# Attention on one core: the order in which TensorE takes scores, transposes and values of the key chunks

## The chip, the cores and the metric

The kernel runs on one core of one Trainium2 chip. The metric is the device time of the whole program in microseconds, the median of several runs. Engines are named as in the profile: PE is TensorE's matmul stream and PEld its weight loads, DVE is VectorE, ACT is ScalarE, POOL is GpSimd, SP is the queue that issues the DMAs here.

## What is computed

One step of a decoder layer with two groups of heads. The part that the change touches is the attention of the 2048 new tokens: four heads, two softmax maps per head, whose difference weighs the values.

```python
def _diff_attend(q, k, v, q_pos, k_pos, lam):
    s = jnp.einsum('bqhmd,bshmd->bhmqs', q.astype(jnp.float32), k.astype(jnp.float32)) * (A_DQK ** -0.5)
    mask = k_pos[None, :] <= q_pos[:, None]
    s = jnp.where(mask, s, -jnp.inf)
    p = jax.nn.softmax(s, axis=-1)
    w = p[:, :, 0] - lam * p[:, :, 1]
    return jnp.einsum('bhqs,bshd->bqhd', w, v.astype(jnp.float32))
```

The sizes: SEQ 2048 in 16 tiles of 128 query rows, 4 heads, 64 columns per map of a query or key, 128 columns of a value, all float32.

## The kernel before

Four passes follow one another, each closed by a barrier of all engines: projections, attention (`pass_attention`), the decoding samples, and the output product. The change lies in the TensorE program of `pass_attention`.

The work is a row of 64 "heads" n = 0 to 63: 16 query tiles in the order of `TILES` (1, 3, ..., 15, then 14, 12, ..., 0; line 939), four heads each. Tile i sees (i + 1) x 128 keys, cut into chunks of up to 512 columns: 1 to 4 chunks; 16 of the 64 heads have 1, 16 have 2, 16 have 3 and 16 have 4. Three stages of the pipeline run in one iteration n:

- `scores(n, c)` (line 1177, matmuls on L1188) makes the scores of chunk c for both maps: six matmuls with 64 rows, three pairs, since float32 is split into a high and a low part (Q_hi K_hi, Q_hi K_lo, Q_lo K_hi). The two maps go to two of four PSUM buffers `sps`, so two chunks fill all four. It waits (L1184) until VectorE has read the two buffers that the chunk before the last one used.
- `weight_columns(n - 3, c)` (line 1193, L1201) transposes the weights of chunk c of head n - 3, 128x128 each, into one of two buffers `tps`; ScalarE copies it to one of two buffers `WT` (`weights_out`, L1087).
- `values(n - 3, c)` (line 1204, L1214) multiplies `WT` with V; each 128x128 block takes two matmul instructions. It waits for ScalarE's copy.

Before the scores of a "prepared" head (`prepared`, line 994: heads 1 to 3 of a tile while K still grows, head 1 later; 29 in all, 22 of them with two or more chunks), `prep` (L1174) transposes a tile of raw K or Q into the next `sps` buffer; ScalarE copies its high part (`split_hi`, L1072) and VectorE the low part (`split_lo`, L1110), which frees the buffer. The wait of `scores(n, 1)` counts this read too.

ScalarE's program in iteration n: `split_hi` of the prepared tile, the exponentials of map 0 of head n - 1 (`exp_row`, L1078), `weights_out(n - 3, 0)`, the exponentials of map 1, then the other `weights_out`. VectorE's: `combine(n - 2)` (L1140, the difference of the two maps over the whole row), `split_lo`, then `rows(n)`: for each chunk and map it reads the scores out of PSUM with scale, mask and running maximum (L1124), and at the end the negated maximum (L1129). Each engine runs its own queue in order.

In the loop at line 1226 TensorE takes, for each c, `scores(n, c)`, `weight_columns(n - 3, c)`, and `values(n - 3, c - 1)`.

Of the kernel before, what the change touches and what calls it, by code (L numbers as in the profile page):

```python
# [941 lines left out]
def pass_attention(nc, io, keep):  # L942


    with ExitStack() as ctx:
# [48 lines left out]
        def prepared(n):  # L994
            u, h = divmod(n, H)
            return tile_raw[u + 1][h - 1:h] if h and u + 1 < NP else ()
# [16 lines left out]
        def n_chunks(n):  # L1013
            return len(chunks[n // H]) if 0 <= n < n_heads else 0
# [11 lines left out]
        @block.sync  # L1026
        def _(sp):
            def load(r):
                if r >= 4:
                    sp.wait_ge(s["sps_full"], raw_use[r - 4] + 1)  # L1030
                kind, t = raw[r]
                sp.dma_start(qk_in[:, r % 4], io["k_p" if kind == "k" else "q_s"][t * P:(t + 1) * P, :]).then_inc(s["qk_load"][r % 4], 16)

            def store(u):
                sp.wait_ge(s["out"], u + 1)
                sp.dma_start(io["o_s"][TILES[u] * P:(TILES[u] + 1) * P, :], ob[:, u % 2]).then_inc(s["store"][u % 2], 16)

            def load_v(q):
                sp.dma_start(V[:, 4 * q:4 * q + 4, :], io["v_p"].rearrange("(b p) n -> p b n", p=P)[:, 4 * q:4 * q + 4, :])\
                  .then_inc(s[f"v_load{q}"], 16)  # L1040

            for r in range(3):
                load(r)
            sp.dma_start(mask[:, :], io["causal"]).then_inc(s["mask_load"], 16)
            load(3)
            load_v(0)
            at = 4
            for u in range(NP):
                if 1 <= u < 4:
                    load_v(u)  # L1050
                while at < len(raw) and at - 4 <= tile_raw[u][-1]:
                    load(at)
                    at += 1
                if u >= 1:
                    store(u - 1)
            store(NP - 1)
            for p in range(2):
                sp.wait_ge(s["store"][p], 16 * NP // 2)
# [107 lines left out]
        @block.tensor  # L1166
        def _(pe):
            def prep(r):
                k = raw_use[r]
                pe.wait_ge(s["qk_load"][r % 4], 16 * (r // 4 + 1))  # L1170
                if k >= 4:
                    pe.wait_ge(s["sps_read"], k - 3)
                for h in range(H):
                    mm = pe.transpose(sps[k % 4][:, h * P:(h + 1) * P], qk_in[:, r % 4, h * P:(h + 1) * P], ident[:, :])  # L1174
                mm.then_inc(s["sps_full"], 1)

            def scores(n, c):

                u, h = divmod(n, H)
                c0, w = chunks[u][c]  # L1180
                if c == 0:
                    pe.wait_ge(s["sps_read"], raw_use[tile_raw[u][-1]] + 1)
                k = first_sc[n] + 2 * c
                pe.wait_ge(s["sps_read"], k - 2)  # L1184
                for q, kk in ((Q_hi, K_hi), (Q_hi, K_lo), (Q_lo, K_hi)):
                    for m in range(2):
                        d = slice(m * DQ, (m + 1) * DQ)
                        mm = pe.matmul(sps[(k + m) % 4][:, 0:w], q[u % 2][d, h, :], kk[d, h, c0:c0 + w],  # L1188
                                       start=(q is Q_hi and kk is K_hi), stop=(q is Q_lo))
                        if q is Q_lo:  # L1190
                            mm.then_inc(s["sps_full"], 1)

            def weight_columns(n, c):
                g = first_wt[n] + c
                if c == 0:
                    pe.wait_ge(s["weights"], n + 1)
                if g >= 2:
                    pe.wait_ge(s["wT"], g - 1)
                c0, w = chunks[n // H][c]
                for b in range(w // P):  # L1200
                    mm = pe.transpose(tps[g % 2][:, b, :], sc[0][:, n % 4, c0 + b * P:c0 + (b + 1) * P], ident[:, :])  # L1201
                mm.then_inc(s["wT_ps"], 1)

            def values(n, c):
                u, h = divmod(n, H)
                g = first_wt[n] + c
                c0, w = chunks[u][c]
                pe.wait_ge(s["wT"], g + 1)
                pe.wait_ge(s[f"v_load{c}"], 16)
                if h == 0 and c == 0 and u >= 2:  # L1210
                    pe.wait_ge(s["out"], u - 1)
                for b in range(w // P):
                    kb = c0 // P + b
                    mm = pe.matmul(ops[u % 2][:, h, :], WT[:, g % 2, b, :], V[:, kb, h * DV:(h + 1) * DV],  # L1214
                                   start=(kb == 0), stop=(kb == TILES[u]))
                mm.then_inc(s["out_ps"], 1)


            for r in tile_raw[0]:
                prep(r)  # L1220
            for n in range(n_heads + 3):
                n_s, n_v = n_chunks(n), n_chunks(n - 3)
                if n < n_heads:
                    for r in prepared(n):
                        prep(r)
                for c in range(max(n_s, n_v + 1)):
                    if c < n_s:
                        scores(n, c)
                    if c < n_v:
                        weight_columns(n - 3, c)  # L1230
                    if 1 <= c <= n_v:
                        values(n - 3, c - 1)


def pass_samples(nc, io, keep):
# [660 lines left out]
```

## Time and profile before

| | |
|---|---|
| median of 3 runs | 1796.92 us (1795.34 to 1799.09) |
| profiled execution: time, span | 1799.58 us, 1797.8 us |
| PE busy in the span | 1609.2 us (90%) |
| PEld busy | 1299.9 us (72%) |
| DVE busy | 988.6 us (55%) |
| ACT busy | 754.3 us (42%) |
| attention stage | 1004.4 to 1394 us of the span |

Busy time is a share of a span with several stages of different limits; the attention stage is read by itself. Matmuls are pipelined, so the cadence of their starts says more than their durations. In a timeline, like instructions in a row are merged: "x4" starts at the first one's start.

### The profile page before, as it was taken

How to read it: one execution, taken by the hardware profiler on the slowest of the kernel's cores; microseconds unless marked ns; L12 is line 12 of the kernel's file. 1: busy time of each engine (PE TensorE's matmuls, PEld its weight loads, DVE VectorE, ACT ScalarE, POOL GpSimd, SP SyncE). 2: the span in 40 equal slices, each digit the busy share in tenths (PEclk: the TensorE clock that was granted, in tenths of full speed). 3: DMA queues.
4: the chain of work that ended last, by engine and by line, in shares of the span. 5: the costliest groups of instructions: out<-in, count | busy, mean ns of one | idle time of the engine just before them, and what ended most of it. 6: DMA issues, size and time to landing. Idle time of an engine off the chain costs nothing. (4 is left out here: it accounts for less than half of the span.)

```text
span 1797.8 us, 25182 instructions
## 1 busy us (share of the span) xinstructions
PE 1609.2 (90%) x9156; PEld 1299.9 (72%) x9156; DVE 988.6 (55%) x2314; ACT 754.3 (42%) x1076; POOL 495.1 (28%) x637
## 2 busy tenths in 40 slices
PE   7799999997999999999999699999998378599998
PEld 5588888886877878788787466777776245377776
DVE  5322222254776676677666498888887341343332
ACT  4333333345445345444544466666666022221110
POOL 1323333333446545644654000000000210012121
PEclk9999999998999999999999699999999589899999
DMA  8433333453001101010110430100000845324342
GB/s 294 173 141 141 141 140 141 175 190 115 30 30 54 36 30 52 31 36 30 54 36 7 152 118 25 47 14 13 13 18 25 254 160 191 107 100 164 134 152 70
DMA packets 79827, 172.27 MB, mean 96 GB/s; under 512 B 9059, under 2 KB 15715, under 8 KB 79715
## 3 DMA queue, kind: packets, MB, share of 16 engines
q1 hardware_dynamic: 79714, 170.79, 27.7%
q8 instruction: 69, 1.13, 0.3%
q14 instruction: 44, 0.35, 0.1%
HBM read 114.13 MB, written 56.62 MB: 95 GB/s over the span
## 5 line engine op out<-in xcount | busy, mean ns | idle before, releaser
L92 PE MATMUL h_banks<-h_w_hi,h_x_hi 128*128 128x512 f32 x1088 | 435.1, 400 | 24.0 <-DVE h_x_lo L651 16.8
L94 PE MATMUL h_banks<-h_w_hi,h_x_lo 128*128 128x512 f32 x1088 | 426.6, 392 | 0.0
L93 PE MATMUL h_banks<-h_w_lo,h_x_hi 128*128 128x512 f32 x1088 | 426.3, 392 | 0.0
L92 PEld LDWEIGHTS h_banks<-h_w_hi,h_x_hi 128*128 128x128 f32 x1088 | 206.3, 190 | 66.6 <-DVE h_x_lo L651 17.2
L94 PEld LDWEIGHTS h_banks<-h_w_hi,h_x_lo 128*128 128x128 f32 x1088 | 205.8, 189 | 44.5
L93 PEld LDWEIGHTS h_banks<-h_w_lo,h_x_hi 128*128 128x128 f32 x1088 | 206.4, 190 | 40.6
L145 POOL TENSOR_TENSOR h_stage_or_levels<-h_stage_or_levels,h_qk_or_hgrn 128x128 f32<-128x128 f32 x192 | 107.4, 559 | 278.2 <-ACT h_stage_or_levels L589 278.2
L1078 ACT ACTIVATE p_scores<-p_scores,p_nmx 128x256 f32<-128x256 f32 (+15 forms) x128 | 153.1, 1196 | 6.2 <-DVE p_nmx L1129 5.9
L1214 PE MATMUL p_ops<-p_V,p_WT 128*128 128x128 f32 x1088 | 146.4, 280 | 8.8 <-ACT p_WT L1087 8.4
L1214 PEld LDWEIGHTS p_ops<-p_V,p_WT 128*128 128x128 f32 x1088 | 132.6, 193 | 15.8 <-ACT p_WT L1087 14.4
L1124 DVE CUSTOM_DVE_ANT_0 p_scores<-p_sps,p_zero 128x512 f32<-128x512 f32 x192 | 122.2, 686 | 15.9 <-PE p_sps L1188 15.7
L737 DVE TENSOR_TENSOR h_qk_or_hgrn<-h_banks,h_mask 128x896 f32<-128x896 f32 x64 | 69.7, 1090 | 105.6 <-PE h_banks L877 105.6
L1087 ACT ACTIVATE p_WT<-p_tps 128x512 f32<-128x512 f32 (+3 forms) x160 | 84.7, 530 | 84.9 <-PE p_tps L1201 84.7
L83 PE MATMUL y_yps<-y_w_hi,y_mT_hi 128*128 128x512 f32 x272 | 111.3, 409 | 7.8 <-DVE y_yt L1764 6.4
L589 ACT ACTIVATE h_stage_or_levels<-h_stage_or_levels 128x2560 f32<-128x2560 f32 x32 | 75.1, 2346 | 102.5 <-DVE h_stage_or_levels L136 102.5
L741 DVE TENSOR_REDUCE h_qk_or_hgrn<-h_qk_or_hgrn 128x128 f32<-128x896 f32 x64 | 111.3, 1739 | 2.2
L876 PE MATMUL h_banks<-h_stage_or_levels 128*128 128x128 f32 x768 | 97.7, 277 | 15.9 <-POOL h_stage_or_levels L150 15.9
L876 PEld LDWEIGHTS h_banks<-h_stage_or_levels 128*128 128x128 f32 x768 | 93.1, 191 | 25.1 <-POOL h_stage_or_levels L150 22.6
L661 DVE TENSOR_REDUCE h_ss<-h_xs_sq_or_tok 128x8 f32<-128x512 f32 x34 | 21.7, 681 | 162.7 <-ACT h_xs_sq_or_tok L486 162.7
L1363 POOL MEMSET s_Q<- 128x1024 f32 x1 | 1.0, 952 | 395.1 <-POOLq L58 395.1
L83 PE MATMUL y_yps<-y_w_lo,y_mT_hi 128*128 128x512 f32 x272 | 108.9, 400 | 0.0
L83 PE MATMUL y_yps<-y_w_hi,y_mT_lo 128*128 128x512 f32 x272 | 108.7, 400 | 0.0
(218 smaller groups left out, 2739.3 us busy)
## 6 DMA issues: line engine op xcount, KB each, us to landing
h_stage_or_levels<-in_w_in SPq DMA_DIRECT2D x32, 512.0 KB, 6.3
h_xs_sq_or_tok<-in_xT SPq DMA_DIRECT2D x17, 512.0 KB, 6.0
h_qk_or_hgrn<-in_x SPq DMA_DIRECT2D x17, 512.0 KB, 6.1
tmp_xh_s<-h_x_hi SPq DMA_DIRECT2D x17, 512.0 KB
tmp_xl_s<-h_x_lo SPq DMA_DIRECT2D x17, 512.0 KB
h_x_hi<-tmp_xh_s SPq DMA_DIRECT2D x17, 512.0 KB, 3.6
h_x_lo<-tmp_xl_s SPq DMA_DIRECT2D x17, 512.0 KB, 4.5
s_kc<-in_cache_k SPq DMA_DIRECT2D x32, 256.0 KB, 3.8
```

The costliest lines, as they stand in the source:

```text
L83: mm = eng.matmul(out, a[:, k, :], b[:, k, cols], start=(k == 0 and a is x_hi and b is w_hi), stop=(k == KD - 1 and a is x_lo))
L92: eng.matmul(out, x_hi[:, k, :], w_hi[:, k, :], start=(k == 0), stop=False)
L93: eng.matmul(out, x_hi[:, k, :], w_lo[:, k, :], start=False, stop=False)
L94: mm = eng.matmul(out, x_lo[:, k, :], w_hi[:, k, :], start=False, stop=(k == KD - 1))
L145: pool.tensor_tensor(e_up, e_up, q_up, ALU.mult)
L589: act.activation(lv[hf], lv[hf], ACT.Exp).then_inc(s["decay"], 1)
L741: dve.tensor_reduce(att[:, h % 2], masked.rearrange("p l t -> p t l"), AX.X, ALU.add).then_inc(s["att"], 1)
L876: pe.matmul(lps[:, n, :], l[:, n, c], l[:, n, c], start=True, stop=True)
L1078: act.activation(row, row, ACT.Exp, bias=nmx[:, n % 2, m:m + 1], accum_out=ls[:, u % 2, m, h:h + 1]).then_inc(s["exp"], 1)
L1087: act.activation(WT[:, g % 2, 0:w // P, :], tps[g % 2][:, 0:w // P, :], ACT.Copy).then_inc(s["wT"], 1)
L1124: dve.tensor_tensor_reduce(sc[m][:, n % (4 - m), c0:c0 + w], sps[k % 4][:, 0:w], add, SCALE, -3e38, ALU.add, ALU.max, mx[:, n % 2, m, c:c ...
L1214: mm = pe.matmul(ops[u % 2][:, h, :], WT[:, g % 2, b, :], V[:, kb, h * DV:(h + 1) * DV], start=(kb == 0), stop=(kb == TILES[u]))
```

## The change

In iteration n, TensorE takes the chunks two at a time: the scores of chunks c0 and c0 + 1 first, then for these two chunks in turn the transposes of head n - 3 and the values of the chunk before. No instruction, buffer or wait differs.

```diff
-                for c in range(max(n_s, n_v + 1)):
-                    if c < n_s:
+                for c0 in range(0, max(n_s, n_v + 1), 2):
+                    for c in range(c0, min(c0 + 2, n_s)):
                         scores(n, c)
-                    if c < n_v:
-                        weight_columns(n - 3, c)
-                    if 1 <= c <= n_v:
-                        values(n - 3, c - 1)
+                    for c in (c0, c0 + 1):
+                        if c < n_v:
+                            weight_columns(n - 3, c)
+                        if 1 <= c <= n_v:
+                            values(n - 3, c - 1)
```

## Rows read from the trace of the kernel before

**Rows 1.** Attention stage's window (busy us per engine, clock, DMA); POOL group, page part 5.
```profile
1004.40:1394.00 389.60, 365.04 (x2720) 278.32 (x2720) 327.20 (x960) 251.66 (x449) 0.00 (x0) 0.97 0.13 43
...
L1363 POOL MEMSET s_Q<- 128x1024 f32 x1 | 1.0, 952 | 395.1 <-POOLq L58 395.1
```
**Rows 2.** Timeline of PE, head 38 (start us, us, engine, line, operation, count).
```profile
1258.47 0.50 PE L1188 MATMUL p_sps<-p_K_hi,p_Q_hi 64*128 64x512 f32 x2
1258.81 0.40 PE L1188 MATMUL p_sps<-p_K_lo,p_Q_hi 64*128 64x512 f32 x2
1259.04 0.39 PE L1188 MATMUL p_sps<-p_K_hi,p_Q_lo 64*128 64x512 f32 x2
1259.36 0.66 PE L1201 MATMUL p_tps<-ident,p_scores 128*128 128x128 f32 x4
1259.95 0.50 PE L1188 MATMUL p_sps<-p_K_hi,p_Q_hi 64*128 64x512 f32 x2
...
1261.34 1.06 PE L1214 MATMUL p_ops<-p_V,p_WT 128*128 128x128 f32 x8
...
1265.56 1.73 PE L1214 MATMUL p_ops<-p_V,p_WT 128*128 128x128 f32 x14
1267.22 0.51 PE L1188 MATMUL p_sps<-p_K_hi,p_Q_hi 64*128 64x512 f32 x2
```
**Rows 3.** Timeline of ACT, head 38: second exponential and the copy after it.
```profile
1260.55 1.67 ACT L1078 ACTIVATE p_scores<-p_scores,p_nmx 128x1664 f32<-128x1664 f32 x1
...
1262.22 0.59 ACT L1087 ACTIVATE p_WT<-p_tps 128x512 f32<-128x512 f32 x1
```
**Rows 4.** Timeline of head 58 (one score chunk, two value chunks), PE and ACT.
```profile
1375.03 0.77 PE L1201 MATMUL p_tps<-ident,p_scores 128*128 128x128 f32 x5
...
1375.72 0.60 ACT L1087 ACTIVATE p_WT<-p_tps 128x512 f32<-128x512 f32 x1 [1.42 <-PE p_tps L1201]
...
1376.37 1.38 PE L1214 MATMUL p_ops<-p_V,p_WT 128*128 128x128 f32 x10 [0.58 <-ACT p_WT L1087]
```
**Rows 5.** Timelines of PE and of DVE, prepared head 22.
```profile
1110.93 0.60 PE L1174 MATMUL p_sps<-ident,p_qk_in 128*128 128x128 f32 x4
...
1112.36 0.66 PE L1201 MATMUL p_tps<-ident,p_scores 128*128 128x128 f32 x4
1113.82 0.50 PE L1188 MATMUL p_sps<-p_K_hi,p_Q_hi 64*128 64x512 f32 x2 [0.80 <-DVE p_K_lo L1110]
...
1115.20 1.06 PE L1214 MATMUL p_ops<-p_V,p_WT 128*128 128x128 f32 x8
...
1111.34 1.82 DVE L1140 SCALAR_TENSOR_TENSOR p_scores<-p_scores,p_coef 128x1536 f32<-128x1536 f32 x1
1113.07 0.69 DVE L1110 TENSOR_TENSOR p_K_lo<-p_sps,p_K_hi 128x512 fp32r<-128x512 f32 x1
```
**Rows 6.** Timeline of PE, prepared head 45: preparation and second chunk's scores.
```profile
1310.52 0.60 PE L1174 MATMUL p_sps<-ident,p_qk_in 128*128 128x128 f32 x4
...
1312.53 0.50 PE L1188 MATMUL p_sps<-p_K_hi,p_Q_hi 64*128 64x512 f32 x2
```
**Rows 7.** Timeline of head 50 (two score chunks), PE and ACT.
```profile
1341.19 0.65 PE L1201 MATMUL p_tps<-ident,p_scores 128*128 128x128 f32 x4
...
1341.89 0.60 ACT L1087 ACTIVATE p_WT<-p_tps 128x512 f32<-128x512 f32 x1 [1.47 <-PE p_tps L1201]
...
1342.38 1.03 ACT L1078 ACTIVATE p_scores<-p_scores,p_nmx 128x896 f32<-128x896 f32 x1
...
1343.41 0.58 ACT L1087 ACTIVATE p_WT<-p_tps 128x512 f32<-128x512 f32 x1
...
1344.04 1.38 PE L1214 MATMUL p_ops<-p_V,p_WT 128*128 128x128 f32 x10
```
**Rows 8.** Page part 5: VectorE's reads of unmasked score chunks.
```profile
L1124 DVE CUSTOM_DVE_ANT_0 p_scores<-p_sps,p_zero 128x512 f32<-128x512 f32 x192 | 122.2, 686 | 15.9 <-PE p_sps L1188 15.7
```
**Rows 9.** View of line 1110: who waited for it (us, times).
```profile
  PEld p_sps L1188: 17.2, 23
```

## The prediction

> **What bounds the kernel now.** I first read the window view of the attention stage: 389.6 us of the 1797.8 us span, TensorE busy 365.04, VectorE 327.20, ScalarE 251.66, no POOL work [rows 1]. POOL's first instruction of the next pass waits 395.1 us at a barrier [rows 1], so no later work overlaps this stage: a microsecond won or lost here counts whole, though the page's chain of waits begins only after the barrier. The change touches nothing else. Then I read the timeline head by head. I write S for the scores of a chunk, T for its transposes, W for ScalarE's copy of T, V for the values, E0 and E1 for the two exponentials; times "at" are from the head's first S.
>
> In the middle of the stage TensorE runs without a hole, but not evenly. In head 38 the pairs of a 512-wide S start 0.34 and 0.23 apart, and T0 0.32 after the third pair [rows 2]. In a steady row each step would be 0.235, so 0.70 for an S; it takes 0.89. T0 to S1 is 0.59 where four transposes at 0.11 make 0.44. So one entry into the 64-row matmuls and one exit cost (0.89 - 0.70) + (0.59 - 0.44) = 0.34. T to V, both 128-row, shows no such cost: fourteen value matmuls and one entry are 1.66 [rows 2], that is 0.11 each and 0.09 for the entry.
>
> The Trainium skill, page "TensorEngine Tiling (Array Packing)", Key Properties, says that changing the tiling mode drains TensorE. The trace agrees with 0.34 per round trip; by that rule alone the change could only gain (last rival).
>
> **The change, part by part.** Before: S0 T0 S1 T1 V0 S2 T2 V1 S3 T3 V2 V3. After: S0 S1 T0 T1 V0 S2 S3 T2 V1 T3 V2 V3. No instruction is added or dropped; no wait is added; the loads and stores on SP's queue and all ScalarE and VectorE queues keep their order and conditions, and move only as their releasers move. Two moves matter: S1 goes ahead of T0 in every head with two or more chunks, and S3 ahead of T2 V1 in four-chunk heads.
>
> *Round trips saved.* Heads with 1, 2, 3 and 4 score chunks: 16 each. S blocks merged: 16x1 + 16x1 + 16x2 = 64. At 0.34 that is 21.8 us, if TensorE is the limit at each and S after S runs at the 0.235 step. No row shows S after S. Bounds: the full 0.34, or nothing (the new S pays the entry again). I take the full saving, since inside an S the pairs already change weights at 0.23.
>
> *T0 to V0.* Now S1 lies between T0 and T1 and hides W0. After, only T1 does. The price stands in head 58, whose order is already T0 T1 V0: T0 at 1375.03, W0 at 1375.72 for 0.60, V at 1376.37 after an idle wait of 0.58 [rows 4]. So V0 is never earlier than T0 + 1.34. Four transposes of T1 fill T0 + 0.93; the rest, 0.41, is a new TensorE hole, and S2 stands queued behind it. In head 38: S1 at 0.81, T0 at 1.60, V0 at 2.94, against V0 at 2.87 now (1261.34 - 1258.47) [rows 2]. The first merge of a head is thus worth -0.34 + 0.41 = +0.07: nothing.
>
> *The second pair (four chunks).* V1 still has S2 S3 T2 ahead of it, V2 has V1 T3; W0 ends at 2.90, E1 (1.67) and W1 (0.59) [rows 3] end about 5.1, V1 is due at 5.65: no hole. S3 moves up to 4.73; VectorE's four reads of chunks 0 and 1 at 0.69 [rows 8] from 0.9 end near 3.7, so the four score buffers are free. Saving 0.34 for a full S3; 0.25 for 128 columns (its tail and T are the same). Net per unprepared four-chunk head about -0.3; of these there are 10 (heads 24, 28, 30-32, 34-36, 38, 39): **-3 us**. In unprepared three-chunk heads (8: 16, 20, 40, 42-44, 46, 47) only +0.07 remains: **+0.6 us**.
>
> *Unprepared two-chunk heads* (8: 8, 12, 48, 50-52, 54, 55). Here ScalarE's queue decides: W0, E1, W1, then V1. In head 50, T0 1341.19, W0 1341.89, E1 1342.38, W1 1343.41, V1 1344.04: V1 follows T0 by 2.85 with ScalarE gapless [rows 7]. No other S lies behind V0 to give slack. T0 moves from 0.89 to 0.81 + 0.62 (a 384-wide S1: 0.70 x 384/512 + 0.09) = 1.43, so V1 and the head's end move by +0.54; with a 128-wide S1 by +0.34. **+3.6 us** at 0.45.
>
> *Prepared heads with two or more chunks* (22). Here the next tile's K or Q transposes come first and take one score buffer; S1's wait asks that VectorE has read it, behind ScalarE's copy and VectorE's combine. Now T0 fills that time, and still S1 waits: the split made TensorE's weight loads wait 23 times, 17.2 us [rows 9]. Head 22: combine from 1111.34, split 1113.07, S1 1113.82 after 0.80 idle, V0 1115.20 [rows 5]. After, T0 stands behind that wait: S1 1113.82, T0 +0.89 = 1114.71, V0 +1.34 = 1116.05: **0.85 later**, the merge gains nothing. Eight three-chunk heads (17-19, 21-23, 41, 45): 6.8 less about 0.3, since 18 and 19 find VectorE a little ahead: +6.5. Eight two-chunk heads (9-11, 13-15, 49, 53) have the 0.85 and ScalarE's E1-W1 chain behind it, about +1.0 each: +8. Six four-chunk heads (25-27, 29, 33, 37): +0.85, less 0.34 for the second pair, less what an earlier S3 gives: VectorE ends its reads sooner and starts the combine sooner, until S1 meets its floor of 2.01 after the preparation, seen in head 45 (1310.52 to 1312.53) [rows 6]; in head 22 it is 2.89 [rows 5], so at most 0.88 can come back. About 0, between -0.4 and +0.5 each. Together **+14.5 us**.
>
> *Sum:* -3 + 0.6 + 3.6 + 14.5 = +15.7 us. The profiled execution is 1799.58 us (span 1797.8 and 1.8 around it), 2.7 above the median 1796.92; so about 1815 for a like profile, and 1796.9 + 15.7 = **1812.6 us** as a median, 0.9% slower.
>
> **Rivals.**
> 1. S after S pays the entry and exit all the same (a matmul's first weight load waits for the semaphore rather than for the mode). Against it: T to V has a semaphore wait too and costs nothing [rows 2]. Then the 10 unprepared four-chunk heads lose 2x0.34, six prepared ones 0.34, 16 other unprepared ones 0.34: +14.3, giving 1827 us.
> 2. The prepared heads lose little: VectorE runs ahead after the earlier scores and S1 always meets its floor. Then heads 13-23 get up to 0.88 back per head, some 10 x 0.8 = 8 us, and if heads 8 to 12 hide their part (some 4 us) behind the loads of the early K tiles, 15.7 - 12 = 3.7 us are left: 1800.6, at the edge of no change.
> 3. Faster: TensorE is the limit everywhere and each of the 64 merges pays 0.34, the drain rule alone: 1796.9 - 21.8 = 1775 us. It needs W0 to be hidden by T1, and T0 not to stand behind S1's wait. It decides at T0 to V0: below 0.93 the gain is whole, at 1.34 it is gone, and head 58 shows 1.34. Partial: if V0 waits but prepared heads lose nothing and two-chunk heads have slack, only the second pairs remain, 16 x -0.34 = -5.4: 1791.
>
> **How the numbers follow.** My forecast (TensorE stops for W0 and for the split) 0.70; rival 1 0.12, slower too; rival 2 0.09, the same; rival 3 with its partial form 0.09, faster. One measurement of this kernel tells about 0.2% (3.6 us) from no change. Slower 0.82, same 0.09, faster 0.09. The range: the bounds of the prepared heads (-8) give 1805 and a little of rival 2 takes it to 1801; rival 1 sets 1826.
>
> **What would show it.** In the profile after: V0's first weight load waiting for p_WT in nearly all 48 heads with two or more chunks, T0 to V0 at 1.34; S1 waiting longer on the split (30 us or more instead of 17.2 us); S to S at 0.81 for full chunks and 0.70 after that; attention stage about 405 us; ScalarE's and VectorE's busy time unchanged. It is wrong if V0 follows T1 without a hole, if T0 slips past the waiting S1, or if full-chunk heads do not shorten by about 0.3.

## The result and the profile after

The changed kernel takes 1815.53 us (median of 4, 1813.19 to 1819.20) beside 1798.01 us before (median of 4): a ratio of 1.0101, interval [1.0076, 1.0126], or 17.5 us slower. The forecast was 15.7 us slower.

From the first transposes of the pass to the end of the last values, the attention stage of the profiled execution grew from 389.05 to 407.45 us, and POOL's wait at the barrier from 395.1 us [rows 1] to 413.5 us: 18.4 us both times (the windows of rows 1 and below are rounded outward). The whole profiled execution is only 13.6 us longer (1813.19 against 1799.58 us), because the passes behind the barrier, whose program is the same, took 398.2 us instead of 404.4 in it (from the end of the last values). TensorE's granted clock explains that: its mean there is 0.92 after and 0.90 before, and PE is busy there for 312.2 us instead of 318.6. Over the kernels of this study that part lies between 398 and 407 us, and the mean clock in it between 0.92 and 0.90. For the mechanism I therefore read the stage, and for the verdict the medians. First the window view of after (columns as in rows 1), then the page's POOL group.

```profile
1005.70:1414.00 408.30, 360.46 (x2720) 283.26 (x2720) 327.77 (x960) 252.13 (x449) 0.00 (x0) 0.97 0.12 41
...
L1364 POOL MEMSET s_Q<- 128x1024 f32 x1 | 1.0, 951 | 413.5 <-POOLq L58 413.5
```

VectorE and ScalarE are busy for the same time as before, with the same instructions; TensorE's busy union even falls by 4.6 us. So nothing became dearer on another engine: 18.4 us are new holes in TensorE's stream less the mode changes saved. The view of waits of TensorE's matmuls in the stage names them (us in total, times, longest). Before:

```profile
PE p_ops L1214 <- ACT p_WT L1087: 8.4, 17, 0.7
PE p_sps L1188 <- DVE p_Q_lo L1110: 6.0, 8, 1.4
PE p_sps L1188 <- DVE p_K_lo L1110: 5.8, 9, 1.2
```

After:

```profile
PE p_ops L1214 <- ACT p_WT L1087: 25.4, 72, 0.7
...
PE p_sps L1188 <- DVE p_Q_lo L1110: 10.2, 13, 1.4
PE p_sps L1188 <- DVE p_K_lo L1110: 9.1, 10, 1.4
```

The values wait 72 times for ScalarE's copy instead of 17 (V0 in all 48 heads with two or more chunks, each time 1.34 to 1.35 behind T0), and S1 waits 19.3 us instead of 11.8 for the split; in weight loads, which rows 9 count, the latter is 17.2 us before and this after (view of line 1110, who waited for it):

```profile
  PEld p_sps L1188: 29.2, 23
```

**An unprepared head.** Head 38 after, TensorE's timeline; it answers to rows 2.

```profile
1270.38 0.50 PE L1188 MATMUL p_sps<-p_K_hi,p_Q_hi 64*128 64x512 f32 x2
1270.72 0.40 PE L1188 MATMUL p_sps<-p_K_lo,p_Q_hi 64*128 64x512 f32 x2
1270.95 0.40 PE L1188 MATMUL p_sps<-p_K_hi,p_Q_lo 64*128 64x512 f32 x2
1271.18 0.40 PE L1188 MATMUL p_sps<-p_K_hi,p_Q_hi 64*128 64x512 f32 x2
...
1271.97 1.09 PE L1201 MATMUL p_tps<-ident,p_scores 128*128 128x128 f32 x8
1273.32 1.16 PE L1214 MATMUL p_ops<-p_V,p_WT 128*128 128x128 f32 x8 [0.25 <-ACT p_WT L1087]
1274.40 0.50 PE L1188 MATMUL p_sps<-p_K_hi,p_Q_hi 64*128 64x512 f32 x2
...
1278.95 0.50 PE L1188 MATMUL p_sps<-p_K_hi,p_Q_hi 64*128 64x512 f32 x2
```

S1 follows S0's last pair after 0.23, the same step as inside an S: the mode change between them is gone. But V0 starts 1.35 after T0 instead of right behind the eight transposes. S0 to V0 is 2.94 (2.87 before). The head ends after 8.57 instead of 8.75 [rows 2].

**A prepared head.** Head 22 after, TensorE and VectorE; it answers to rows 5.

```profile
1122.04 0.60 PE L1174 MATMUL p_sps<-ident,p_qk_in 128*128 128x128 f32 x4
...
1124.93 0.50 PE L1188 MATMUL p_sps<-p_K_hi,p_Q_hi 64*128 64x512 f32 x2 [1.39 <-DVE p_K_lo L1110]
...
1125.82 1.09 PE L1201 MATMUL p_tps<-ident,p_scores 128*128 128x128 f32 x8
1127.16 1.16 PE L1214 MATMUL p_ops<-p_V,p_WT 128*128 128x128 f32 x8 [0.25 <-ACT p_WT L1087]
...
1122.45 1.82 DVE L1140 SCALAR_TENSOR_TENSOR p_scores<-p_scores,p_coef 128x1536 f32<-128x1536 f32 x1
1124.18 0.68 DVE L1110 TENSOR_TENSOR p_K_lo<-p_sps,p_K_hi 128x512 fp32r<-128x512 f32 x1
```

S1 starts 2.89 after the preparation, exactly as before, since VectorE's combine and split end when they did. T0 no longer fills that time: the hole grows from 0.80 to 1.39, T0 comes after S1, and V0 is 5.12 after the preparation instead of 4.27 [rows 5].

**A two-chunk head.** Head 50 after, TensorE and ScalarE; it answers to rows 7.

```profile
1358.08 1.09 PE L1201 MATMUL p_tps<-ident,p_scores 128*128 128x128 f32 x8
...
1360.93 1.38 PE L1214 MATMUL p_ops<-p_V,p_WT 128*128 128x128 f32 x10 [0.24 <-ACT p_WT L1087]
...
1358.77 0.60 ACT L1087 ACTIVATE p_WT<-p_tps 128x512 f32<-128x512 f32 x1 [2.29 <-PE p_tps L1201]
1359.26 1.03 ACT L1078 ACTIVATE p_scores<-p_scores,p_nmx 128x896 f32<-128x896 f32 x1
...
1360.29 0.75 ACT L1087 ACTIVATE p_WT<-p_tps 128x512 f32<-128x512 f32 x2
```

T0 to V1 is 2.85, as it was [rows 7]: copy, exponential, copy without a gap. T0 is 0.53 later in the head, so V1 and the head's end are.

By classes of heads, the change in the length of a head (from its first TensorE instruction to the next head's), summed over the class, beside the terms of the forecast:

```
class of heads                   count   forecast   measured
unprepared, 4 chunks               10      -3.0       -2.4
unprepared, 3 chunks                8      +0.6       +1.4
unprepared, 2 chunks                8      +3.6       +3.4
prepared, 4 chunks                  6       0         +0.9
prepared, 3 chunks                  8      +6.5       +7.7
prepared, 2 chunks                  8      +8.0       +8.1
the rest (1 chunk, start, end)     19       0         -0.7
sum, us                                   +15.7      +18.4
```

In all heads with two or more chunks TensorE's granted clock is 1.00 in both profiles, so these classes compare like with like. The -0.7 of the rest goes with the clock, not with the order: at the start of the stage the clock is 0.50 until 1026.7 us before, and it is back at 1.00 from 1016.6 to 1020.0 us after, where head 3 is 0.8 shorter.

### The profile page after: what moved, and what is told of

It reads as the page before. It is cut to its first block and busy times, and to the rows that moved or that the text cites. A ratio compares the mean times of both kernels' runs of the same rounds, so it can differ in the third digit from the quotient of the medians.

```text
span 1811.4 us, 25182 instructions
## 1 busy us (share of the span) xinstructions
PE 1598.5 (88%) x9156; PEld 1300.8 (72%) x9156; DVE 976.4 (54%) x2314; ACT 752.5 (42%) x1076; POOL 499.8 (28%) x637
## 5 line engine op out<-in xcount | busy, mean ns | idle before, releaser
L92 PE MATMUL h_banks<-h_w_hi,h_x_hi 128*128 128x512 f32 x1088 | 435.3, 400 | 26.5 <-DVE h_x_lo L651 18.4
L1214 PE MATMUL p_ops<-p_V,p_WT 128*128 128x128 f32 x1088 | 151.9, 285 | 25.8 <-ACT p_WT L1087 25.4
L1364 POOL MEMSET s_Q<- 128x1024 f32 x1 | 1.0, 951 | 413.5 <-POOLq L58 413.5
L876 PE MATMUL h_banks<-h_stage_or_levels 128*128 128x128 f32 x768 | 97.7, 277 | 14.8 <-POOL h_stage_or_levels L150 14.8
```

What stands on the lines that cost most here:

```text
L92: eng.matmul(out, x_hi[:, k, :], w_hi[:, k, :], start=(k == 0), stop=False)
L876: pe.matmul(lps[:, n, :], l[:, n, c], l[:, n, c], start=True, stop=True)
```

## The experiments

All eight kernels keep every instruction; only the order in one engine's queue or two changes. The stage is given from the start of the first transposes of the pass to the end of the last values, read off the timeline: 389.05 us before, 407.45 after. The diffs are cut to the lines that make the difference; unless said otherwise they are against the changed kernel.

**1. The second pair alone.** Chunks 0 and 1 in the old order.

```diff
-                for c0 in range(0, max(n_s, n_v + 1), 2):
...
+                for c0 in (0, 1, 2):
+                    group = (c0,) if c0 < 2 else (2, 3, 4)
```

> Only chunks 2 and 3 are paired; chunks 0 and 1 keep the old order. My theory: the second pair gains a mode round trip of 0.25 to 0.34 in each of 16 four-chunk heads and costs nothing, since V1 and V2 have enough ahead of them: -4 to -6 us against before, about 1793 us, and V0 of the 48 heads starts where it did before. Rival (pairing as such is what costs: it bunches VectorE's reads and TensorE waits for score buffers): slower than before by 2 us or more, with S2 or S3 waiting for VectorE's reads.

Measured: 1787.68 us (median of 9) beside 1799.98, ratio 0.9949 [0.9926, 0.9972]; stage 381.10, 8.0 below before. The direction is that of the theory, and the heads with fewer than four chunks are unchanged to 0.3 us in sum. The size is above it: the ten unprepared four-chunk heads give -3.7 us, as expected, but the six prepared ones give -4.4, up to 1.03 each (head 29) instead of 0.34. There S3, which now comes ahead of T2 and V1, lets VectorE end its reads and begin the next head's combine sooner, and the split that S1 asks for is done sooner: in head 29 the combine starts 1.09 ahead of S0 instead of 0.12, and S1 follows S0 at 1.65 instead of 2.63. The waits of this kernel show it too, 8.8 us where before had 11.8:

```profile
PE p_sps L1188 <- DVE p_K_lo L1110: 4.7, 9, 0.8
PE p_sps L1188 <- DVE p_Q_lo L1110: 4.1, 6, 1.4
```

So bunching the scores does not hurt as such: in the second pair four full score buffers are no bottleneck.

**2. The first pair alone.**

```diff
-                for c0 in range(0, max(n_s, n_v + 1), 2):
+                for group in ((0, 1), (2,), (3,), (4,)):
```

> Only chunks 0 and 1 are paired. My theory: all of the loss sits here, and the small gain of the second pair is missing: 4 to 6 us above the changed kernel, about 1820 us. Rival (bunching costs): about the changed kernel's 1815 us or below, since half of the bunching is gone.

Measured: 1829.36 us (median of 4), ratio 1.0161 [1.0114, 1.0208]; stage 423.31, 15.9 above the changed kernel's where 4 to 6 was expected. The whole loss does sit in the first pair, as the theory says, but two things were missing. The second pair is worth 8 us, not 5 (run 1). And in this profile TensorE's granted clock fell to half in heads 26 and 27 and again, near the end of the stage, in heads 60 to 63. The window view shows the first time (columns: window, us, then busy us of PE, PEld, DVE, ACT and POOL, granted clock, DMA share, GB/s), and the timeline what came just before it:

```profile
1155.00:1162.00 7.00, 5.25 (x42) 3.85 (x40) 6.17 (x18) 2.80 (x5) 0.00 (x0) 0.98 0.00 0
1162.00:1163.50 1.50, 1.48 (x7) 1.18 (x6) 0.47 (x2) 1.50 (x2) 0.00 (x0) 0.50 0.00 0
1163.50:1165.00 1.50, 1.50 (x9) 1.18 (x9) 0.00 (x0) 1.02 (x3) 0.00 (x0) 0.50 0.00 0
1165.00:1166.50 1.50, 1.50 (x14) 1.14 (x11) 0.83 (x3) 0.24 (x1) 0.00 (x0) 0.96 0.00 0
```

```profile
1160.08 0.50 PE L1188 MATMUL p_sps<-p_K_hi,p_Q_hi 64*128 64x512 f32 x2 [1.75 <-DVE p_K_lo L1110]
...
1162.32 2.08 PE L1214 MATMUL p_ops<-p_V,p_WT 128*128 128x128 f32 x8
```

Head 26 has a hole of 1.75 us in front of S1, then the wait of V0; the clock goes to 0.50, that is 1.2 GHz, and eight value matmuls take 2.08 instead of 1.16. Heads 26 and 27 lose 2.2 and 2.1 us here instead of the 0.95 of the other prepared heads, heads 60 to 63 another 4.2 us, although their order is not changed at all: some 6.7 us by the clock, and 8.6 by the missing second pair (the last 0.6 lie at the start of the stage, in head 3 above all). The four executions fit: 1835.22 and 1838.78 us with a mean granted clock of 0.958 and 0.959, 1822.45 and 1823.50 us with 0.966 and 0.968. The latter two are 7 and 8 us above the changed kernel, about what the second pair is worth in run 1.

**3. The change without the first pair in prepared heads.**

```diff
+                first = ((0,), (1,)) if n < n_heads and prepared(n) else ((0, 1),)
+                for group in (*first, (2, 3), (4,)):
```

> As the change, but in the 29 prepared heads chunks 0 and 1 keep the old order, so that T0 again fills the wait for the split of the prepared tile. My theory: the 22 prepared heads with two or more chunks, which lost 16.7 us in the trace, come back to before or 0.3 below it (second pair): about 1798 us, within 3 us of before; the unprepared two-chunk heads keep their +3.5 us. Rival (the new wait of V0 for ScalarE's copy is the whole cost, in all 48 heads): only the copy's wait of about 0.5 comes back in 22 heads, 11 us at most, and 1804 us or more are left.

Measured: 1795.70 us (median of 10) beside 1799.98, ratio 0.9976 [0.9956, 0.9995]; stage 385.20, 22.3 below the changed kernel. The theory's case, a little better. The prepared three-chunk heads are back at before (0.0 in sum), the prepared four-chunk heads at -4.2 (run 1's gain), the unprepared classes where the change put them (+3.5, +1.5 and -2.5 for two, three and four chunks); the prepared two-chunk heads are 1.5 below before. The rival, that only V0's wait comes back there, would have left 1804 us or more. The waits for the split are down to 7.9 us, those of the values still 17.1, now in the unprepared heads:

```profile
PE p_ops L1214 <- ACT p_WT L1087: 17.1, 46, 0.7
...
PE p_sps L1188 <- DVE p_Q_lo L1110: 4.3, 6, 1.4
PE p_sps L1188 <- DVE p_K_lo L1110: 3.6, 7, 0.8
```

**4. Pairs, but T0 first:** T0 S0 S1 T1 V0 S2 S3 T2 V1 T3 V2 V3.

```diff
+                if n_v:
+                    weight_columns(n - 3, 0)
                 for c0 in range(0, max(n_s, n_v + 1), 2):
                     for c in range(c0, min(c0 + 2, n_s)):
                         scores(n, c)
                     for c in (c0, c0 + 1):
-                        if c < n_v:
+                        if 0 < c < n_v:
                             weight_columns(n - 3, c)
```

> As the change, but T0 goes ahead of S0 and S1: T0 S0 S1 T1 V0 S2 S3 T2 V1 T3 V2 V3. The same 64 merged blocks of scores, but two blocks of scores and T1 lie between T0 and V0, and T0 does not stand behind the wait of S1. My theory: the saved mode changes now show: -0.34 per merge in unprepared heads (36 merges, -12 us), -0.3 in the prepared four-chunk heads, something in the one-chunk heads where S0 hides ScalarE's copy (up to -5 us): 13 to 19 us below before, 1779 to 1785 us. Rival (merging scores saves nothing that lasts, VectorE or ScalarE limits the stage): within 4 us of before.

Measured: 1775.55 us (median of 6) beside 1799.98, ratio 0.9870 [0.9843, 0.9896]: by the medians 24.4 us faster than before and some 40 faster than the change, with the same 64 merged blocks; stage 368.27, 20.8 below before. The theory's case, counted here from a head's first scores to the next head's: -5.8, -2.8 and -3.6 us in the unprepared heads of four, three and two chunks (12.2 together, 12 expected), -4.5 in the prepared four-chunk ones, -5.1 in the one-chunk heads. Of these last 5.1 some 3 us cannot be put down to the order: they lie in heads 3 to 5, where the granted clock was at 1.00 from 1019.9 us on, and before only from 1026.7. Head 38 again, TensorE:

```profile
1245.12 0.60 PE L1201 MATMUL p_tps<-ident,p_scores 128*128 128x128 f32 x4
1245.65 0.49 PE L1188 MATMUL p_sps<-p_K_hi,p_Q_hi 64*128 64x512 f32 x2
...
1247.24 0.66 PE L1201 MATMUL p_tps<-ident,p_scores 128*128 128x128 f32 x4
1247.73 1.06 PE L1214 MATMUL p_ops<-p_V,p_WT 128*128 128x128 f32 x8
1248.72 0.50 PE L1188 MATMUL p_sps<-p_K_hi,p_Q_hi 64*128 64x512 f32 x2
```

V0 follows T1 at 0.49 without a hole, 2.61 behind T0, and S2 follows V0 after 0.99; in the changed kernel it was 1.08 (1273.32 to 1274.40). So a waiting V0 costs not only the wait of 0.41 but 0.1 more in its first matmul (the second starts 0.21 behind it instead of 0.11), the term that the forecast lacked. No run puts T0 first without pairing the scores, so what T0's place alone is worth is not shown.

Still waiting in this kernel is S1, 13.2 us for the split. Four more orders tried to take that away or to refine the change.

**5. The preparation one block earlier,** ahead of the last values of the head before (beside run 4's lines).

```diff
-                if n < n_heads:
+                if n <= 3:
                     for r in prepared(n):
                         prep(r)
...
+                        if c == n_v and 3 <= n < n_heads - 1:
+                            for r in prepared(n + 1):
+                                prep(r)
                         if 1 <= c <= n_v:
                             values(n - 3, c - 1)
```

> As e4_columns_first, but the transposes of a prepared tile go ahead of the last values of the head before, so that the split has the time of one block of values more (0.2 to 0.9 us) before S1 asks for it. My theory: in e4 the wait of S1 for the split is what keeps the prepared heads from gaining (13.2 us of matmul waits): most of it goes where the combine was not the later one, -5 to -10 us against e4, about 1767 us. Rival (S1 waits for VectorE's combine, not for the preparation): within 2 us of e4's 1775.6 us.

Measured: 1774.51 us (median of 4) beside 1797.63, ratio 0.9861 [0.9804, 0.9919]; stage 370.43. The expected 5 to 10 us did not come; the rival's case. The waits for the split are 12.6 us. In head 22, S1 is 1.92 behind S0, as in run 4, for VectorE's combine (1.82) stands ahead of the split in its queue, and an earlier preparation does not move that. Only the prepared four-chunk heads gain by it (-6.3 instead of run 4's -4.5), while early in the stage the preparation itself now waits for a score buffer (2.5 us instead of 0.2). The stage is 2.2 longer than run 4's because heads 60 to 66 are 2.5 longer: the granted clock was 0.50 there from 1363.1 us on, and in run 4 only from 1368.1.

**6. The changed kernel with the second copy ahead of the second exponential** in ScalarE's queue.

```diff
-                if n_chunks(n - 3):
-                    weights_out(n - 3, 0)
+                for c in range(min(2, n_chunks(n - 3))):
+                    weights_out(n - 3, c)
                 if 1 <= n <= n_heads:
                     exp_row(n - 1, 1)
-                for c in range(1, n_chunks(n - 3)):
+                for c in range(2, n_chunks(n - 3)):
```

> The changed kernel, with ScalarE's order altered: the copy of the second transposed chunk goes ahead of the second exponential. My theory: in two-chunk heads V1 waits for W0, E1 and W1 in a row, which is the part of their loss beyond the wait of V0: the unprepared ones lose 1 us instead of 3.4, the prepared ones 5 instead of 8, so 4 to 6 us below the changed kernel, about 1810 us. Rival (V1 waits for nothing of ScalarE's order; the heads lose by V0 alone): the same as the changed kernel, 1815 us.

Measured: 1814.74 us (median of 9), ratio 1.0084 [1.0055, 1.0112]; stage 404.63, 2.8 below the changed kernel. Head by head the theory holds: unprepared two-chunk heads lose 0.5 instead of 3.4 us, prepared ones 5.9 instead of 8.1. But one-chunk heads 5 and 6, early in the stage, lose 2 us more than in the changed kernel's profile. That is not the edit, which changes ScalarE's order only from iteration 11 on, where the first head with two chunks has its weights copied. What differs there is the granted clock, 1.00 in the changed kernel's profile and still 0.50 in this one (the same stretch, first after, then this run):

```profile
1026.80:1032.60 5.80, 4.85 (x34) 3.23 (x34) 5.55 (x17) 4.38 (x11) 0.00 (x0) 1.00 0.00 0
1026.80:1032.60 5.80, 5.33 (x22) 3.14 (x20) 4.00 (x11) 2.92 (x8) 0.00 (x0) 0.50 0.00 1
```

The two-chunk heads alone gain 5.1 us, within the 4 to 6 expected, but the medians (1814.74 and 1815.53) do not tell the two kernels apart. The chain of ScalarE is shown as the cause in these heads; a gain of the whole is not.

**7. Runs 5 and 6 together** (both diffs).

> e5_early_prep with the ScalarE order of e6_copy_first: both together. Theory: 0 to 4 us below e5, since T0 first leaves ScalarE more time already. Rival: the later second exponential delays VectorE's combine and the split: slower than e5 by 2 us or more.

Measured: 1777.72 us (median of 4), ratio 0.9883 [0.9820, 0.9946]; stage 369.63, 0.8 below run 5. Heads 60 to 66 alone are 2.3 shorter than in run 5, by the clock; the medians do not tell the two apart. With T0 first, ScalarE's order no longer matters much.

**8. Run 5 with VectorE's split ahead of its combine** (beside run 5's lines).

```diff
+                if n < n_heads:
+                    for r in prepared(n):
+                        split_lo(r)
                 if 2 <= n < n_heads + 2:
                     combine(n - 2)
                 if n < n_heads:
-                    for r in prepared(n):
-                        split_lo(r)
                     rows(n)
```

> e5_early_prep, with VectorE's order altered: in a prepared head the split's low part goes ahead of the combine instead of behind it. Theory after e5: S1 waits for VectorE's combine (1.8 us in head 22), which stands ahead of the split; with the early preparation the split is ready before the combine starts, so S1 follows S0 at 0.8 and the 12.6 us of TensorE's waits for the split in e5 go, less what the later combine makes S2 wait: 5 to 10 us below e5, 1765 to 1770 us. Rival (the combine holds back the reads of the first chunk anyway, so S2 waits where S1 did): within 3 us of e5's 1774.5 us.

Measured: 1781.22 us (median of 6) beside 1799.11, ratio 0.9921 [0.9893, 0.9949]; stage 371.35, 0.9 above run 5, and 3.2 above it without heads 60 to 66, which the clock made longer in run 5. The rival's mechanism, though the median is 6.7 above run 5's and so outside the 3 us that the rival allowed: S1 now follows S0 at 0.80 in head 22, and S2 waits instead, for the reads that stand behind the combine. The waits changed their name and kept their size, with 1.4 us for the split left (line numbers are one higher here):

```profile
PE p_sps L1189 <- DVE p_mx L1124: 12.2, 22, 1.1
```

In prepared heads, then, what is left is VectorE's own work: combine, split and the first reads in a row, which TensorE needs at one point or the next.

## Why the prediction was right

- *What bounds the stage.* Right: 18.4 us in the stage are 18.4 us at the barrier, with the other engines' work unchanged.
- *Round trips saved, 0.34 each, S after S at the 0.235 step.* Right, although no row of before showed S after S: 0.23 in head 38 after. Rival 1 (the entry is paid all the same) falls with it. Run 4, where the same merges stand without the new waits, gives 0.33 to 0.38 in each of the eight unprepared three-chunk heads and 0.70 in four-chunk heads such as 38.
- *T0 to V0 never below 1.34.* Right: 1.34 to 1.35 in all 48 heads with two or more chunks. The price was mis-sized: 0.41 for the hole, without the slower first matmul behind it. Unprepared three-chunk heads lost 0.13 to 0.25 instead of 0.07 (+1.4 against +0.6), prepared three-chunk heads mostly 0.95 instead of 0.85 (+7.7 against +6.5).
- *Prepared heads: T0 stands behind the wait of S1.* Right, and the largest term. Run 3 takes it away, together with V0's wait in the same heads, and gets 22 us back, twice the 11 that V0's wait alone could give at most (22 heads at about 0.5). In the four-chunk heads the balance was +0.9, not 0: in run 2 the first pair costs the four of them that ran at full clock 0.95 to 1.04 each, where 0.85 was counted (V0's extra tenth again), and the second pair gives 0.5 to 1.2 of it back.
- *Two-chunk heads: W0, E1, W1 in a row.* Right to 0.2 us in both classes, and run 6 shows the cause by altering that order alone.
- *The second pair.* Right in the unprepared heads (-3.7 in run 1, where 10 x 0.3 was counted); in the prepared ones it is worth 0.35 to 1.03, all beyond 0.34 through VectorE, which the forecast had weighed as "at most 0.88" and netted to nothing.
- *Rival 3, faster.* It named T0 to V0 as the point that decides. Run 4 is that rival made true by another order: with V0's wait and S1's place changed the stage is 20.8 us shorter, and 21.8 us was this rival's sum. That the two are so near is chance: the heads with merged blocks give 14.8 of it, since the prepared two-chunk heads still lose 1.8, and the one-chunk heads, with no merge, give 5.1, some 3 of them where the clock differs. *Rival 2* asked for VectorE to run ahead in the prepared three-chunk heads; it does not, because the combine keeps its place (S1 2.89 behind the preparation before and after).
- Of the signs named beforehand, the attention stage was set at about 405 us (408.3), the waits on the split at 30 us or more (29.2), S to S at 0.81 (0.80).

What stays open: what T0 first is worth without pairs, and how far the falls of the clock vary from one execution of a kernel to the next.

## What to carry to other kernels

Before grouping work of one kind to save mode changes on an in-order engine, write down what each moved block was hiding: here the scores between T0 and V0 hid a copy of 0.6 us on ScalarE, and T0 hid a wait of S1, and both were worth more than the 0.34 saved. Look for the order that groups and still starts the other engine's job first: moving T0 ahead of the pair turned +17.5 us into -24.4 us with the same instructions. A wait that changes its name when its releaser is moved (run 8) marks the engine that sets the time at that place.

## What was not expected of the hardware

- Going from the 128-row matmuls into the 64-row ones and back costs TensorE 0.34 us in all, and it is saved in full when two such blocks follow one another (0.23 from S0's last pair to S1), even with a semaphore wait in front of the second, as long as that is already met.
- A block of values that had to wait ends 0.1 us later than its length (1.08 instead of 0.99 to the next block).
- The granted clock fell from 1.00 to 0.50 in run 2 behind holes of 1.75 and 1.74 us in heads 26 and 27, and was at 0.50 for 3.4 us each time. The length of a hole alone does not tell: the clock stayed at 1.00 through holes of 1.4 us in the changed kernel (heads 22 and 23), of 1.65 in head 29 of run 2 and of 2.0 in head 9 of run 8, and in head 60 of run 2 it fell behind waits of 0.58 that the kernel before has too, at 1.00.
